# Two low-part activation buffers moved 32 bytes against their high parts, in a matmul-bound transformer kernel

## The reference, cut to what matters

```python
def swiglu(h, w_gate, w_up, w_down):
    return (jax.nn.silu(h @ w_gate) * (h @ w_up)) @ w_down

q = (h @ w_q).reshape(B, S, MEM_HEADS, MEM_HEAD_DIM)
hn = rms_norm_2(h, ffn_pre_norm)
u = causal_dwconv(hn @ w_up, conv_w, conv_b)
gate, up = jnp.split(u, 2, axis=-1)
y = (jax.nn.gelu(gate, approximate=True) * up) @ w_down
```

## The kernel before, in words

| buffers | before | changed |
|---|---|---|
| raw, whi, wlo (all six) | 128 | 128 |
| X, SQ, Hhi, held | 832 | 832 |
| Hlo | 832 | 864 |
| H2, MEM, FH, KVr, MKV | 832 | 832 |
| EW | 832 | 832 |
| FL, A, cst | 832 | 864 |
| R, TG / TU / SG, E, PT, rope, ones | 928 / 960 / 992 | 960 / 992 / 0 |
| nw / rt | 736 / 480 | 768 / 512 |

## Time and profile before

### The profile page before, as it was taken

The page is one execution under the profiler, slowest core; times in us unless marked ns, Lnnn a source line. Parts: engine busy times, 40 slices in busy tenths (PEclk is TensorE's granted clock), DMA queues, the critical chain, the costliest instruction groups (busy, mean ns, idle before and its releaser), DMA issues.

```text
span 1194.2 us, 24046 instructions
## 1 busy us (share of the span) xinstructions
PE 1144.7 (96%) x9142; PEld 1088.0 (91%) x9142; DVE 876.8 (73%) x1480; ACT 612.3 (51%) x1072; POOL 64.3 (5%) x53
## 2 busy tenths in 40 slices
PE   9999999999999999998999999999979799999997
PEld 8988898999999999778989999999967599999997
DVE  6999886676666687556768666657897857999954
ACT  6754555544445544344445444454455745666542
POOL 0677000000000000000000000000000000000000
PEclk9999999999999999999999999999989989999999
DMA  8554443355555656124524555565553213455562
GB/s 286 177 189 164 141 162 121 128 191 190 196 188 199 212 188 226 63 72 162 207 70 170 189 189 195 177 212 196 210 181 107 71 41 124 172 183 198 181 212 106
DMA packets 32008, 198.42 MB, mean 166 GB/s; under 512 B 3776, under 2 KB 6080, under 8 KB 9024
## 3 DMA queue, kind: packets, MB, share of 16 engines
q1 hardware_dynamic: 29440, 193.09, 46.8%
q10 hardware_dynamic: 2496, 4.33, 1.1%
HBM read 194.12 MB, written 1.05 MB: 163 GB/s over the span
## 4 chain that ended last, share of the span: by engine, by line
PE 74%; DVE 17%; ACT 3%; issue 3%; DMA 1%; ACTq 0%; DVEq 0%; SPq 0%
PE acc L491 21%; PE acc L492 20%; PE acc L493 20%; DVE sc L1923 4%; PE acc L507 2%; DVE wlo L1456 2%; PE acc L774 2%; DMA raw<-weights 1%; PE acc L527 1%; DVE wlo L1451 1%; PE sc L738 1%; PE st L642 1%; PE tp L763 1%; ACT whi L1004 1%; DVE mx L1833 1%
## 5 line engine op out<-in xcount | busy, mean ns | idle before, releaser
L491 PE MATMUL acc<-Hhi,whi 128*128 128x256 f32 x1368 | 384.3, 281 | 5.3 <-DVE wlo L1456 5.2
L492 PE MATMUL acc<-Hlo,whi 128*128 128x256 f32 x1368 | 381.1, 279 | 0.0
L493 PE MATMUL acc<-Hhi,wlo 128*128 128x256 f32 x1368 | 381.1, 279 | 0.0
L1004 ACT ACTIVATE whi<-raw 128x1024 fp32r<-128x1024 f32 x160 | 169.4, 1059 | 335.1 <-PE acc L493 304.3
L1451 DVE TENSOR_TENSOR wlo<-raw,whi 128x1024 fp32r<-128x1024 f32 (+1 forms) x158 | 193.6, 1225 | 106.0 <-ACT whi L1004 105.6
L491 PEld LDWEIGHTS acc<-Hhi,whi 128*128 128x128 f32 x1368 | 257.8, 188 | 7.6 <-DVE wlo L1456 4.4
L493 PEld LDWEIGHTS acc<-Hhi,wlo 128*128 128x128 f32 x1368 | 258.7, 189 | 0.0
L492 PEld LDWEIGHTS acc<-Hlo,whi 128*128 128x128 f32 x1368 | 256.8, 188 | 0.2
L1456 DVE TENSOR_TENSOR wlo<-raw,whi 128x1024 fp32r<-128x1024 f32 (+1 forms) x158 | 193.3, 1223 | 1.6 <-ACT whi L1007 0.3
L491 PE MATMUL acc<-FH,whi 128*128 128x256 f32 x608 | 170.6, 281 | 5.2 <-DVE FH L2086 3.3
L493 PE MATMUL acc<-FH,wlo 128*128 128x256 f32 x608 | 169.5, 279 | 0.0
(11 more groups left out here) (356 smaller groups left out, 2007.5 us busy)
## 6 DMA issues: line engine op xcount, KB each, us to landing
raw<-weights SPq DMA_DIRECT2D x177, 1024.0 KB, 4.9
MEM<-mem_in SPq DMA_DIRECT2D x2, 1024.0 KB, 7.3
held<-weights SPq DMA_DIRECT2D x2, 1024.0 KB, 5.9
E<-A ACTq DMA_DIRECT2D x12, 128.0 KB, 2.4
X<-x_in ACTq DMA_DIRECT2D x4, 256.0 KB, 6.1
raw<-weights SPq DMA_DIRECT2D x4, 256.0 KB, 6.9
MEM<-consts ACTq DMA_DIRECT2D x2, 512.0 KB, 4.9
out<-MKV SPq DMA_DIRECT2D x4, 256.0 KB, 2.1
```

Source lines behind the costliest of these rows:

```text
L491: pe.matmul(dst, w, x, start=first, stop=False)
L492: pe.matmul(dst, w, xl, start=False, stop=False)
L493: return pe.matmul(dst, wl, x, start=False, stop=last)
L1004: act.activation(whi[j][:, 0:HALF, 0:width], raw[j][:, 0:HALF, 0:width], ACT.Copy).then_inc(hi_out, 1)
```

## The change

Three fillers are added in the list of SBUF tensors, and nothing else.

```diff
         with ExitStack() as shared:
-            Hhi, Hlo = sb("Hhi", [P, DC, S], F32R, shared), sb("Hlo", [P, DC, S], F32R, shared)
+            Hhi = sb("Hhi", [P, DC, S], F32R, shared)
+            sb("apart_low", [P, 4], F32, shared)
+            Hlo = sb("Hlo", [P, DC, S], F32R, shared)
         held = [sb(f"held{j}", [P, KC, MB]) for j in range(2)]
+        sb("apart_pair", [P, 256])
         with ExitStack() as shared:
             H2 = sb("H2", [P, 2, DC, S], F32R, shared)
         H2hi, H2lo = H2[:, 0, :, :], H2[:, 1, :, :]
...
             KVr = sb("KVr", [P, 4 * DC, S], F32R, shared)
         MKV = sb("MKV", [P, 4 * DC, S])
+        sb("apart_gated", [P, 4])
         with ExitStack() as shared:
             FL = sb("FL", [P, FC, S], F32R, shared)
         A = sb("A", [P, FC, S])
```

## The result

The changed kernel is slower: 1210.01 us in the median of 4 runs (1206.06 to 1211.29) against 1193.32 us of 4 runs of the kernel before beside it (1189.19 to 1195.82). The ratio on record is 1.0113, with a 95% interval of 1.0079 to 1.0147; it is not the quotient of the two medians, which is 1.0140 and lies inside the interval. The forecast was 1179 us, 1.1% faster than before, with a range of 1174 to 1207 us; the measured time lies above the range. The profiled execution has a span of 1208.9 us where the one before had 1194.2 us.

A forecast was written before the change was run, and what follows sets the result against it. TensorE's matmul pace was taken as the bound: -11.7 us from plain stretches and -1.5 us from turned ones, -13.2 us or 1.1% off the 1192.29 us median, gave 1179 us, range 1174 to 1207 us.

The forecast's parts named there:

- What bounds the kernel: Whole kernel: TensorE busy for 96% of the span, so the pace of `three`'s matmuls goes into the time nearly one for one.
- That places matter at all: Last two tiles of `wout`: operands at an equal place modulo 1024 take 120.0 ns against 113.3 ns, 6.7 ns a matmul.
- The two paces of the kernel before: Stretches of `three`: the same matmul runs at 113.3 ns (346.49 us listed) or 117.8 ns (388.57 us listed), start to end.
- no effect: Rival, chance 0.30: a stretch's starting moment chooses its pace, 32 bytes don't enter; 1192 us, give or take 5.
- the choice of ends: Stretches of `three`: plain ones at 117.8 ns go to 113.3 ns, turned ones half; no loss at 113.3 ns; together -13.2 us.
- -11.7 us for the plain stretches: Plain stretches at 117.8 ns: 2631 matmuls go to the shorter pace, 4.45 ns off each, 11.7 us gained.
- One overlap of three goes from 704 to 736 bytes: Plain triples reading `Hlo` or `FL`: loading `wlo` under the moving operand is the only new relation; 1368 and 352 triples.
- Everywhere else in `three` the operand pair lies 704 bytes apart: Outside `wout`'s last two tiles: one distance modulo 1024 between moving and loaded operand, at 113.3 or 117.8 ns.
- The turned stages: Turned stretches at 117.8 ns, 78.68 us, 668 matmuls: half of a possible 3.0 us taken, -1.5 us.
- the mechanism of the forecast: Triples of `three`: spoiling one of three like relations acts first on the longer pace, which needs the three; 4.45 ns a matmul.
- The slower rival: Chance 0.28: loading `wlo` under `Hlo`/`FL` comes nearer a bad place and costs time; from 1199 us up, to 1220 us.
- Priced at nothing: Vector work and full-precision matmuls at places moved 32 bytes: no cost, records staying at 686, 684 and 379 ns.

The follow-up runs named there:

- e5: All activations, high and low, moved 64 bytes further on against the kernel before (896, distance 768 from the weights); 1222.33 us, ratio 1.0241.
- e8: The kernel before, unchanged, profiled a second time; one run, 1190.23 us, `gu0` and `gu1` both 138.5 us.
- e2: The change, with the low weights `wlo` moved by 32 bytes too, so every load lies 704 from its stream; 1212.88 us, ratio 1.0160.
- e3: As the change, but `Hlo` and `FL` moved by 64 bytes (896) instead of 32; 1207.80 us, ratio 1.0112 to the kernel before.
- e7: As the change, but `Hlo` and `FL` moved by 128 bytes (960) instead of 32; 1207.50 us, ratio 1.0106 to the kernel before.
- e13: As the change, but `Hlo`, `FL` and the weights `wlo` all moved by 64 bytes, every distance 704; 1212.11 us, ratio 1.0153 to the kernel before.
- e1: All activations, high and low, moved 32 bytes further on against the kernel before (864, distance 736), no jump between streams; 1211.09 us, ratio 1.0136.
- e6: All activations moved 128 bytes further on against the kernel before (960, distance 832 from the weights); 1209.49 us, ratio 1.0137.
- e14: All activations at 288 modulo 1024 instead of the kernel before's 832, distance 160 from the weights; 1212.11 us, ratio 1.0157.
- e15: All activations at 256 modulo 1024 instead of the kernel before's 832, distance 128 from the weights; 1215.29 us, ratio 1.0183.
- e9: All activations at 576 modulo 1024 instead of the kernel before's 832, distance 448 from the weights; 1193.44 us, ratio 1.0009.
- e12: Against the kernel before, high activations at 320, low ones 512 bytes further on (832), distances 192 and 704; 1193.94 us, ratio 1.0000.

## Why the prediction was wrong, point by point

**What bounds the kernel** was right. TensorE's busy time and the span moved together, the costliest groups wait for the same releasers as before, and VectorE and ScalarE have their old totals within 0.8 us.

**That places matter at all**, read off the 120.0 ns of the earlier trace rows, was right. e5 made the whole kernel run at 120.0 ns by a uniform distance of 768. The Trainium skill, "SBUF — State Buffer", section "Who interferes with whom", gives TensorE two independent read ports and says that it never waits on anyone. By that, every kernel of the table would have stayed at 1192 us, and the runs disagree: fifteen kernels with other places gave ratios from 0.9989 to 1.0241, and eleven of them have an interval clear of 1.

**The two paces of the kernel before** were read rightly, and e8 shows what the forecast gave as an argument for no effect: equal places, and a stretch takes either pace.

**The step that failed** is the choice of ends: "the best end for the stretches at 117.8 ns and no loss for those at 113.3 ns", with its reason, "a shift that spoils one of three like relations acts first on the pattern that needs the three". It is the other way round. The shift broke the shorter pace, and did not free the stretches at the longer one: every jump of 32, 64 or 128 bytes (the change, e2, e3, e7, e13) and every distance off 192 (e1, e5, e6, e14, e15) took the 113.3 ns from both long stretches. The forecast's -11.7 us for the plain stretches was instead a loss in both kinds: at 118.9 ns each matmul costs 5.6 ns more than at 113.3 ns and 1.1 ns more than at 117.8 ns. By the listed stretches that are plain this is 3058 x 5.6 ns = 17.1 us and 2631 x 1.1 ns = 2.9 us, 20.0 us if the change reached all of them. Of the triples with `H2` and with `FH` as low part, which it does not reach, 283 took 340 ns in the trace of before; without them it is 15.2 us. The rest of the 17.2 us of busy time lies outside the listed stretches and is not itemised.

**A term that the forecast did not have** is the jump between streams. "One overlap of three goes from 704 to 736 bytes" is all that it counts as new; that the streamed operand now starts at 832, 864 and 832 in turn was priced at nothing, without a reason. e2 put every overlap back to 704 and left the jump, and the pace was 119.1 ns; e1 has the distance of 736 without the jump, and 118.3 ns. Either is enough to lose the shorter pace.

**One distance for both orders** was also misread. "Everywhere else in `three` the operand pair lies 704 bytes apart" leaves out which operand streams: modulo 256 it is 192 in a plain stage and 64 in a turned one. At 64 the plain stages of e6 never kept the shorter pace for a long stretch.

**The turned stages** were to give 1.5 us. Their pace in the change is that of the longer kind. In `down2` the groups of lines 496 and 497 have 280 ns (1150 to 1180 us), as at 117.8 ns before, so nothing was gained. e8 shows that the same stage can run at 113.3 ns with no change at all.

**The place of the gain that did come** is small: in the third tile of `wout`, where `Hhi` and `Hlo` stream over `FH`, the groups of lines 495 and 496 fell from 283 ns to 280 ns (992.5 to 1001 us):

```profile
L496 PE MATMUL acc<-KVr,FH 128*128 128x256 f32 x8 | 2.3, 282 | 0.0
...
L496 PE MATMUL acc<-Hlo,FH 128*128 128x256 f32 x8 | 2.2, 280 | 0.0
L495 PE MATMUL acc<-Hhi,FH 128*128 128x256 f32 x8 | 2.2, 280 | 0.0
```

One of three relations left the distance 0 there, and the triple got shorter, on 8 triples. That fits the mechanism of the forecast, in the one place where the kernel before stood at the worst distance and not at the best.

**The slower rival** (0.28) had the right sign and half of the mechanism: the overlap at 736 costs (e1), but it too had no price for the jump (e2). It sized one triple at 340.0 + 6.7 = 346.7 ns, 1199 us, then all at 117.8 ns, 1206 us, and all at 120.0 ns, 1220 us. Measured are 356.7 ns and 1210 us, between its last two. The range ended at 1207 us because "everything at 117.8 ns" was taken as its upper end; it should have ended at 120.0 ns.

**Priced at nothing, and rightly:** vector work and full-precision matmuls at moved places, against the earlier trace rows:

```profile
L1708 DVE TENSOR_TENSOR TU<-TU,SG 128x512 f32<-128x512 f32 x22 | 15.1, 684 | 0.0
L1694 DVE TENSOR_TENSOR FL<-TU,FH 128x512 f32 x20 | 13.7, 684 | 0.0
```

```profile
L742 PE MATMUL sc<-MKV,A x64: 379/379/483, 191.7 to 615.2; 128*128 128x256 f32 x64
```

## What to carry to other kernels

Where fp32r matmuls of 256 columns follow each other with a new load each, count the places of the streamed and of the loaded operand modulo 256 bytes before moving a buffer: here, in the plain order, 192 was the good distance, 0 the worst, and all streams that take turns had to start alike modulo 256. In the turned order neither rule is shown beyond the cost of 0. A filler of 32, 64 or 128 bytes in front of an operand was not free here, and one of 256 or 512 bytes was. Profile such a kernel more than once, since stretches of the same code may take one of two paces from one execution to the next; a single profile gave 143.9 us for a stage that took 138.5 us in the next.

## What the runs showed of the hardware that was not expected

- The fp32r triples of this kernel keep their mean pace for over a thousand matmuls. At the distance 192 modulo 256 (704, 448, 192, and mixed with jumps of 256 and 512) the plain stretches `gu0` and `gu1` of six profiles took 138.5 us ten times and 143.9 us twice. At every other distance, and with every jump that is no multiple of 256, both stretches of a profile took the same time to 0.01 us.
- The sign of the distance seems to count, but it is not proven. At 64 modulo 256 the plain stretches of e6 took 143.9 us both times. The turned `down2` is at 64 in six profiles with `FH` and `FL` alike modulo 256: its long stretch had the longer pace in five (the first of before and e9 to e12; 56.30 us in the first) and the shorter one in e8 (54.18 us). At 192, in e6, it had the shorter one, while `diffv` had the longer in all these seven. Giving turned stages the distance 192 too was not tried by itself; on the 668 matmuls of the two long turned stretches it could be worth 3.0 us at most.
- A distance of 0 modulo 256 is felt by fp32r matmuls (120.0 ns against 113.3 ns) and not by full-precision ones. The same piece of line 527 (`raw` loaded, `MEM` streamed), 175 matmuls of 216 ns, first in the kernel before (distance 704), then in e5 (768):

```profile
86.69:124.46 37.77, 37.77 (x176) 1.00 0.46 155
86.87:124.64 37.77, 37.77 (x177) 1.00 0.46 155
```

- What in the memory or in the array makes 256 bytes the period is not shown by any run here. That in the plain order a jump and a distance cost separately is shown (e2, e13, and e1); how they add up in the change's 118.9 ns is not taken apart further.
